# Weight pieces: rests written in place, four load buffers, loads issued one piece earlier in order

## The reference, cut to what matters

```python
# first network, each of 2 layers
h = x @ w_in                       # split: MLA, stick-breaking, forgetting and memory attention, gates, merge
y = four attention branches; merged = sum_n sigmoid(merge_r @ w_merge_up)[n] * ((y[n] * silu(gate[n])) @ w_branch[n])
x = layer_norm(ALPHA * x + merged @ w_out)
# second network, each of 2 layers
h = rmsnorm(x, norm_g[l])
z = h @ w_in_2[l]                  # q, k, v, gate of the four branches a, b, c, d
q_a, k_a = axial_rope(rmsnorm(q_a)), axial_rope(rmsnorm(k_a));  o_a = dense attention
q_b, k_b = rope(q_b), rope(k_b);                                o_b = attention in a window, with a sink
o_c = neighbourhood attention on a grid, with a table of biases rpb_c[l]
q_d, k_d = rope(q_d), rope(k_d);                                o_d = differential attention
x = x + concat(o * silu(gate)) @ w_out_2[l]
```

## Time and profile before

| | |
|---|---|
| median of 3 runs | 1443.2 us (1442.56 to 1445.12) |
| the profiled execution | 1443.2 us, span of its instructions 1441.4 us |
| mean granted TensorE clock | 0.988 of full speed |
| TensorE busy | 1371.9 us (95%) |
| VectorE, ScalarE, GpSimd busy | 864.6 (60%), 732.6 (51%), 382.0 us (27%) |
| transfers on SyncE's queue | 30.9% of the 16 DMA engines' time |
| chain that ended last | TensorE 72%, VectorE 14%, ScalarE 7% |

### The profile page before, as it was taken

One profiled execution on the slowest core, in us unless ns is written; L12 is line 12 of the kernel. 1 busy time (PEld: TensorE's weight loads), 2 busy tenths in 40 slices (PEclk: granted clock), 3 DMA queues, 4 the chain that ended last, 5 costly groups with the idle time before them and its releaser, 6 DMA issues.

```text
span 1441.4 us, 20050 instructions
## 1 busy us (share of the span) xinstructions
PE 1371.9 (95%) x7466; PEld 1064.1 (74%) x7466; DVE 864.6 (60%) x1513; ACT 732.6 (51%) x1561; POOL 382.0 (27%) x273
## 2 busy tenths in 40 slices
PE   7999999999989999999998899999899999999897
PEld 7877788778787777887776777776766877675665
DVE  4656536557662564455577675568656665578555
ACT  4555447655344554556554464446444554546443
POOL 2233131346131322213554111421012111421111
PEclk9999999999999999999999999999999999999999
DMA  7413551125353221112265532511323443511311
GB/s 236 118 31 92 115 142 48 52 72 224 102 161 65 55 88 59 59 48 66 77 229 167 130 74 59 125 59 52 103 67 90 111 93 70 113 59 23 118 51 59
DMA packets 185894, 135.65 MB, mean 94 GB/s; under 512 B 91334, under 2 KB 166726, under 8 KB 185798
## 3 DMA queue, kind: packets, MB, share of 16 engines
q1 hardware_dynamic: 182022, 120.22, 30.9%
q10 hardware_dynamic: 3776, 14.16, 2.5%
HBM read 122.03 MB, written 12.32 MB: 93 GB/s over the span
## 4 chain that ended last, share of the span: by engine, by line
PE 72%; DVE 14%; ACT 7%; issue 2%; POOL 2%; DMA 1%; SPq 1%; DVEq 0%; ACTq 0%; POOLq 0%
PE pb L1650 18%; PE pb L1652 17%; PE pb L1651 17%; PE pb L1741 5%; PE pb L1690 5%; PE pb L1717 5%; ACT prob L1797 3%; ACT tmp L1797 2%; DVE prob L2420 2%; DVE wl L2167 2%; SPq L2698 1%; PE pb L1772 1%; DMA tbias<-zscr 1%; PE pb L1726 1%; POOL wl L2564 1%
## 5 line engine op out<-in xcount | busy, mean ns | idle before, releaser
L2564 POOL TENSOR_TENSOR wl<-wr,wh 128x512 fp32r<-128x512 f32 x178 | 253.5, 1424 | 706.3 <-ACT wh L1817 702.1
L1650 PE MATMUL pb<-xh,wl 128*128 128x512 f32 (+1 forms) x880 | 350.2, 398 | 11.9 <-DVE wl L2167 6.4
L1652 PE MATMUL pb<-xh,wh 128*128 128x512 f32 (+1 forms) x880 | 324.8, 369 | 0.0
L1651 PE MATMUL pb<-xl,wh 128*128 128x512 f32 (+1 forms) x880 | 324.3, 369 | 0.0
L2167 DVE TENSOR_TENSOR wl<-wr,wh 128x512 fp32r<-128x512 f32 x208 | 167.2, 806 | 175.3 <-ACT wh L1817 175.1
L1817 ACT CAST wh<-wr 128x512 fp32r<-128x512 f32 (+1 forms) x386 | 220.1, 606 | 36.2 <-PE pb L1652 22.1
L1650 PEld LDWEIGHTS pb<-xh,wl 128*128 128x128 f32 x880 | 167.3, 190 | 65.6 <-issue 29.5
L1652 PEld LDWEIGHTS pb<-xh,wh 128*128 128x128 f32 x880 | 167.1, 190 | 29.1
L1651 PEld LDWEIGHTS pb<-xl,wh 128*128 128x128 f32 x880 | 167.9, 191 | 24.6 <-issue 4.3
L1797 ACT ACTIVATE tmp<-pb,cst 128x512 f32<-128x512 f32 (+3 forms) x128 | 83.0, 648 | 72.3 <-PE pb L1652 26.8
L1650 PE MATMUL pb<-wh,xl 128*128 128x256 f32 (+1 forms) x320 | 109.2, 341 | 10.9 <-DVE wl L2167 8.0
(11 more groups left out here) (198 smaller groups left out, 2339.0 us busy)
## 6 DMA issues: line engine op xcount, KB each, us to landing
wr<-w_in SPq DMA_DIRECT2D x39, 1024.0 KB, 5.3
wr<-w_out SPq DMA_DIRECT2D x14, 1024.0 KB, 5.1
wr<-w_in SPq DMA_DIRECT2D x48, 256.0 KB, 4.5
wr<-w_branch SPq DMA_DIRECT2D x48, 128.0 KB, 2.3
x<-prob SPq DMA_DIRECT2D x12, 512.0 KB, 3.6
wr<-w_mem_kv SPq DMA_DIRECT2D x4, 1024.0 KB, 5.8
prob<-x ACTq DMA_DIRECT2D x2, 2048.0 KB, 10.6
wr<-w_out SPq DMA_DIRECT2D x16, 256.0 KB, 4.2
```

The source lines that it names most:

```text
L1650: e.matmul(ps, ll, rh, start=start, stop=False)
L1651: e.matmul(ps, lh, rl, start=False, stop=False)
L1652: t = e.matmul(ps, lh, rh, start=False, stop=stop)
L2564: t = e.tensor_tensor(wl[:, j % 2, c0:c1], wr[:, j % 2, c0:c1], wh[:, j % 2, c0:c1].bitcast(F32), ALU.subtract)
```

## The change

The buffers of the loaded pieces and of the rests become one: the subtraction writes the rest over the loaded values. There are four of these buffers (`j % 4`), laid over each other as `wr` (float32) and `wl` (rounded format); the high parts keep two (`j % 2`). The memory taken is the same. Since TensorE reads the rest where the load was, the load of piece j waits for the last product with piece j - 4, and for nothing else. One more load is put at the start (`wload` after the first features), so behind the last cast of piece j stands the load of piece j + 3. The loads have four semaphores in place of two.

```diff
+N_LOADED, N_HIGH = 4, 2
@@ plan
     tick()
     run(second)
+    wload()
@@ build
-    wr = sb("wr", [P, 2, 2048])
-    wh, wl = sb("wh", [P, 2, 2048], F32R), sb("wl", [P, 2, 2048], F32R)
+    with nc.sbuf_tensor("wr", [P, N_LOADED, 2048], F32) as wr:
+        pass
+    wl, wh = sb("wl", [P, N_LOADED, 2048], F32R), sb("wh", [P, N_HIGH, 2048], F32R)
...
-    d_w = [signal(f"d_w{i}", 16) for i in range(2)]
+    d_w = [signal(f"d_w{i}", 16) for i in range(N_LOADED)]
...
+    def loaded(j, c0, c1):
+        return wr[:, j % N_LOADED, c0:c1]
@@ scalar_program, cast
-                    w.wait_ge(d_w[j % 2], d_w[j % 2].at(j))
+                    w.wait_ge(d_w[j % N_LOADED], d_w[j % N_LOADED].at(j))
...
-                w.wait_ge(gemm, gemm.at(("w", j - 2)))
-                e.copy(wh[:, j % 2, c0:c1], wr[:, j % 2, c0:c1]).then_inc(w_hi.sem, w_hi.mark((j, c)))
+                w.wait_ge(gemm, gemm.at(("w", j - N_HIGH)))
+                e.copy(wh[:, j % N_HIGH, c0:c1], loaded(j, c0, c1)).then_inc(w_hi.sem, w_hi.mark((j, c)))
@@ vector_program and gpsimd_program, cast
-                t = e.tensor_tensor(wl[:, j % 2, c0:c1], wr[:, j % 2, c0:c1], wh[:, j % 2, c0:c1].bitcast(F32), ALU.subtract)
+                hi = wh[:, j % N_HIGH, c0:c1].bitcast(F32)
+                t = e.tensor_tensor(wl[:, j % N_LOADED, c0:c1], loaded(j, c0, c1), hi, ALU.subtract)
@@ sync_program, load
-                if j >= 2:
-                    c = n_chunks(j - 2) - 1
-                    w.wait_ge(w_lo, w_lo.at((j - 2, c - c % 2)))
-                    w.wait_ge(w_lo2, w_lo2.at((j - 2, c - 1 + c % 2)))
-                    w.wait_ge(w_hi, w_hi.at((j - 2, c)))
-                v = wr[:, j % 2, 0:kc * n].rearrange("p (k c) -> p k c", k=kc)
+                w.wait_ge(gemm, gemm.at(("w", j - N_LOADED)))
+                v = loaded(j, 0, kc * n).rearrange("p (k c) -> p k c", k=kc)
```

More of the change, by code:

```diff
@@ L1491, in weights @@
         _, kc, n = WEIGHTS[j][0:3]
-        return (wl if lo else wh)[:, j % 2, 0:kc * n].rearrange("p (k c) -> p k c", k=kc)
-    def n_chunks(j):
-        return -(-WEIGHTS[j][1] * WEIGHTS[j][2] // 512)
+        part = wl[:, j % N_LOADED, 0:kc * n] if lo else wh[:, j % N_HIGH, 0:kc * n]
+        return part.rearrange("p (k c) -> p k c", k=kc)
+    def loaded(j, c0, c1):
+        return wr[:, j % N_LOADED, c0:c1]
     def pieces_of(j):
@@ L2618, in sync_program @@
             elif k == "load":
-                j, g = s["j"], d_w[s["j"] % 2]
+                j, g = s["j"], d_w[s["j"] % N_LOADED]
                 name, kc, n = WEIGHTS[j][0:3]
-                if j >= 2:
-                    c = n_chunks(j - 2) - 1
-                    w.wait_ge(w_lo, w_lo.at((j - 2, c - c % 2)))
-                    w.wait_ge(w_lo2, w_lo2.at((j - 2, c - 1 + c % 2)))
-                    w.wait_ge(w_hi, w_hi.at((j - 2, c)))
-                v = wr[:, j % 2, 0:kc * n].rearrange("p (k c) -> p k c", k=kc)
+                w.wait_ge(gemm, gemm.at(("w", j - N_LOADED)))
+                v = loaded(j, 0, kc * n).rearrange("p (k c) -> p k c", k=kc)
                 for (k0, k1), (c0, c1), src, (p0, p1) in pieces_of(j):
```

## The result

The kernel after takes 1470.4 us (median; 1469.2 to 1473.8), the one before 1443.6 beside it (1442.6 to 1445.1): ratio 1.018, 95% interval 1.016 to 1.019. It is 27 us slower; the forecast was 1460 with a range to 1467. The profiled execution has a span of 1469.2 us against 1441.4.

The account below looks back on a forecast made before the run. TensorE, busy 1371.9 us (95%), was taken as the bound. Tables 5.6 and 2.5, biases 4.2 and clock 5.0 sum to 17.3 us, less 0.5, on 1443.2: forecast 1460 us, range 1449 to 1467.

Parts of the forecast that it names:

- Place by place ... every weight load still goes out before its old time: Weight loads in SyncE's queue: none goes out later than before, smallest lead 4.0 us, so no cast is late.
- At two kinds of places another transfer is: SyncE's queue behind moved loads: only A's rope tables and C's biases, in both layers, are late at a cost.
- Earlier loads, value 0, best end a gain of 3: ScalarE's three waits for loads, 11.6 us in all: loading earlier gains 0, at best 3 us.
- Term 1: Rope tables of A, layer 0: read 8.4 us late, stalling TensorE 5.6 us at a rest of `Akv`; bounds 4.0 and 7.9.
- lesser case: Layer 0 tables not travelling behind load and stores: landing at 834.1 instead of 835.6, stall 1.5 us less.
- Term 2: Rope tables of A, layer 1: 4.7 us late, stalls of 1.9 and 0.6, together 2.5 us; bounds 1 and 4.
- Term 3: C's biases, both layers: 2.1 us late each, stalling TensorE at `Dq`'s first rest, 4.2 us together; bounds 3 and 5.
- Term 4, the clock: TensorE's clock falls to half after three long new stalls, losing 1.65 us each: 5.0 us; bounds 0 and 6.6.
- What is late but costs nothing: Stores of x wait up to 16 us longer, at no cost; their slots are rewritten later.
- bare stalls: Rival, chance 0.2: TensorE's clock stays up after the new stalls, adding 12.3 us, 1455.5 us in all.
- layer 0 alone: Rival, chance 0.12: only A's layer 0 tables cost, layer 1 and biases are covered; 5.6 + 1.7, 1450.5 us.
- The second: Rival, chance 0.06: late transfers are covered by VectorE's idle time and earlier loads pay 3 us, 1440 us.

Follow-up runs that it names:

- all three first: Kernel after, with the spreads, A's tables and C's biases each put ahead of the load they followed in SyncE's queue: 1441.5 us, ratio 0.997 to the kernel before.
- at the old places: Kernel after without the one added `wload()` call, so each load stands at its old place in SyncE's queue: 1441.8 us, ratio 0.998 to the kernel before.
- the biases first: Kernel after, with only C's bias transfers put ahead of the load they followed in SyncE's queue: 1465.9 us, ratio 1.013 to the kernel before.
- only the tables late: Kernel after, with spreads and biases put ahead of their loads and A's tables left behind theirs: 1457.8 us, ratio 1.009 to the kernel before.

## Why the prediction was wrong

The direction (forecast with a chance of 0.93) and the kind of cause (transfers behind a waiting load) were right; the time was 10 us too small, outside the range. By its steps:

- *"Place by place ... every weight load still goes out before its old time", no cast late*: right. One wait of 3.3 us is left of three.
- ***"At two kinds of places another transfer is"*: the step that failed.** There are three. The spreads were left out, 5.9 us in the traces, 5.1 by the medians or 6.1 by the ratios when undone. The row was there: VectorE's wait of 6.1 us for `zscr<-scr` in the waits of before, a reader that already waits for a transfer which the same helper puts behind the loads. The forecast listed stores, tables and biases, the same that the description of SyncE's order names, and didn't go through all that stands behind a load.
- *Earlier loads, value 0, best end a gain of 3*: wrong in sign. Once `Aq` comes early, GpSimd's rest of it falls upon VectorE's chain, 0.75 us in after and 0.93 with all three first; the bounds had only gains. The step near 790 in after is 2.4 us with the half clock that moved; the stall grew from 3.02 to 4.26 us where TensorE ran at full clock just before it and came sooner. With all three first nothing of it shows in the median.
- *Term 1*, 5.6 of stall and 1.65 of clock: 5.70 of stall and 2.5, since the half clock lasted 6.8 us, 4.8 of it behind the stall. First read at 844.6, which is 835.6 plus the 9.0 already late: the working was right to 0.1 us, and the runs show its parts (issues, and a landing later behind other bytes). Only its lesser case, tables that don't travel behind the stores and the load, was taken from the first table's issue; from the second, 0.8 us later, it would be 0.7 us less and not 1.5, which moves the range's lower end by under 1 us.
- *Term 2*, 2.5: 2.6, with the full clock kept, as taken.
- *Term 3*, 4.2 and two falls of the clock, 7.5: 3.9 + 4.4 = 8.3. The stalls grew by 2.3 and 2.8 in place of 2.1 each.
- *Term 4, the clock*, 5.0: mis-sized. It is 8.4 over the whole kernel: 1.4 behind the missed spreads, a stretch twice as long at 848 and at 797, others that only shifted. The forecast took a fall behind a long stall as sure; in after the clock stays full behind the very stall that it had for this (2.74 us at 782 in before, 2.75 at 788.7 in after).
- *"What is late but costs nothing"*, the stores: right.

With the two missed places (5.9 and 2.4) the forecast's 16.8 would be 25.1 of 27.8. Of the rivals, bare stalls was wrong as to the clock, and layer 0 alone as to layer 1's tables and the biases. The second, a gain from covered transfers, is what the same buffers give at the old places, though by way of the biases.

## What to carry to other kernels

To move a waiting DMA forward in an in-order queue, first list each transfer that stands behind it until its old place, with its reader and the reader's slack; helpers that issue two kinds at once are to be included. Here the same tables sent out 11.7 us late were free, and cost 8 us with a load and two stores between their wait and them. Where small transfers whose own waits end earlier can stand ahead of a load that waits, put them there: it gave some 3 us here (4.5 to 5 by the ratios) with no memory spent. An earlier load is an earlier cast and an earlier subtraction, and can fall on the engine that is late.

## What the runs showed that was not expected

- The landing time of two tables of the same size in layer 0: 2.6 to 2.9 us with nothing ahead, 3.9 to 4.4 behind a load's four issues, 5.1 to 6.0 behind the load and two stores.
- The clock fell to half behind stalls of 2.70 us (at 214) and 3.5 and more, and not behind 2.25 us (at 1174), while in the run with the biases first it fell behind 1.95 us (at 426) and 2.18 (at 1173). Nor did it fall behind the 2.75 us at 788.7 in after, where before it fell behind 2.74. The length of the stall alone doesn't tell.
- Executions of one kernel spread over 2 to 11 us, and the longer ones mostly have the lower mean granted clock: the kernel before took 1438.6 us at 0.993 and 1449.4 at 0.986. A profiled execution can lie 7 us off its median, as with only the tables late; single terms under 3 us are read from the steps of a trace, not from a median.
